# Two of three down projections of the second FFNs: one plain pair of lots, then three pairs in seven half products

## The reference, cut to what matters

```
def swiglu(x, w1, w3, w2):
    return (jax.nn.silu(x @ w1) * (x @ w3)) @ w2
...
for l in range(DEPTH):                       # DEPTH = 2, D_MODEL = 1024, D_FF = 2816
    x = x + 0.5 * swiglu(rms_norm(x, ffn1_norm[l]), ffn1_w1[l], ffn1_w3[l], ffn1_w2[l])
    ... mixing ...
    x = x + 0.5 * swiglu(rms_norm(x, ffn2_norm[l]), ffn2_w1[l], ffn2_w3[l], ffn2_w2[l])
```

## Time and profile before

| | us |
|---|---|
| span of the profiled execution | 2748.1 |
| median of the executions timed | 2749.83 |
| lowest, highest of 3 | 2749.41, 2750.02 |
| TensorE busy | 2743.3 (100%) |
| TensorE weight loads busy | 2337.2 (85%) |
| VectorE busy | 1851.7 (67%) |
| ScalarE busy | 1335.1 (49%) |
| GpSimd busy | 940.7 (34%) |

### The profile page before, as it was taken

One profiled execution on the slowest core, in us unless ns is written; L12 is line 12 of the kernel. 1 busy time (PEld: TensorE's weight loads), 2 busy tenths in 40 slices (PEclk: granted clock), 3 DMA queues, 4 the chain that ended last, 5 costly groups with the idle time before them and its releaser, 6 DMA issues.

```text
span 2748.1 us, 41845 instructions
## 1 busy us (share of the span) xinstructions
PE 2743.3 (100%) x16054; PEld 2337.2 (85%) x16054; DVE 1851.7 (67%) x2984; ACT 1335.1 (49%) x2103; POOL 940.7 (34%) x466
## 2 busy tenths in 40 slices
PE   9999999999999999999999999999999999999999
PEld 8898888777788889898998988887777888898988
DVE  7686857885667448585785878578846674585755
ACT  6353444655355346353563534446553653553533
POOL 0135824433343442131121357244333434421221
DMA  5333583222222232233332335832222222322332
GB/s 171 108 108 116 151 180 107 84 71 72 83 85 85 85 100 94 92 116 100 108 108 92 116 115 159 171 108 84 70 73 81 86 83 85 100 99 94 108 98 102
DMA packets 113110, 284.80 MB, mean 104 GB/s; under 512 B 35617, under 2 KB 45345, under 8 KB 112417
## 3 DMA queue, kind: packets, MB, share of 16 engines
q1 hardware_dynamic: 112928, 282.35, 34.6%
HBM read 268.67 MB, written 9.44 MB: 101 GB/s over the span
## 4 chain that ended last, share of the span: by engine, by line
PE 99%; DVE 1%; ACT 0%; issue 0%; DVEq 0%; ACTq 0%
PE bank L627 22%; PE bank L629 22%; PE bank L628 22%; PE bank L676 7%; PE bank L677 7%; PE bank L678 7%; PE bank L653 1%; PE bank L655 1%; PE bank L654 1%; PE bank L1048 1%; PE bank L1067 1%; PE bank L1082 1%; PE bank L817 1%; PE bank L1181 1%; PE bank L1035 0%; PE bank L1240 0%
## 5 line engine op out<-in xcount | busy, mean ns | idle before, releaser
L476 POOL TENSOR_TENSOR w_lo<-raw,w_hi 128x1024 fp32r<-128x1024 f32 x208 | 519.8, 2504 | 872.1 <-ACT w_hi L468 872.1
L627 PE MATMUL bank<-h_hi,w_hi 128*128 128x512 f32 x1504 | 593.4, 395 | 0.5 <-DVE silu_a L2363 0.3
L629 PE MATMUL bank<-h_hi,w_lo 128*128 128x512 f32 x1504 | 585.8, 390 | 0.0
L628 PE MATMUL bank<-h_lo,w_hi 128*128 128x512 f32 x1504 | 585.8, 390 | 0.0
L468 ACT ACTIVATE w_hi<-raw 128x1024 fp32r<-128x1024 f32 x310 | 326.5, 1056 | 353.8 <-PE bank L629 313.5
L541 POOL TENSOR_TENSOR w_lo<-raw,w_hi 128x1024 fp32r<-128x1024 f32 x122 | 223.4, 1854 | 802.3 <-DVE bank L2308 802.3
L627 PEld LDWEIGHTS bank<-h_hi,w_hi 128*128 128x128 f32 x1504 | 282.3, 188 | 65.6 <-issue 7.1
L629 PEld LDWEIGHTS bank<-h_hi,w_lo 128*128 128x128 f32 x1504 | 282.4, 188 | 59.8
L628 PEld LDWEIGHTS bank<-h_lo,w_hi 128*128 128x128 f32 x1504 | 282.5, 188 | 56.4
L627 PE MATMUL bank<-g_hi,w_hi 128*128 128x512 f32 x698 | 271.9, 390 | 0.0
L628 PE MATMUL bank<-g_lo,w_hi 128*128 128x512 f32 x698 | 271.7, 389 | 0.0
(11 more groups left out here) (452 smaller groups left out, 5895.7 us busy)
## 6 DMA issues: line engine op xcount, KB each, us to landing
raw<-in_w_lots SPq DMA_DIRECT2D x478, 512.0 KB, 3.7
s_wd<-s_z SPq DMA_DIRECT2D x8, 512.0 KB, 2.7
s_t<-s_taps SPq DMA_DIRECT2D x16, 256.0 KB, 12.9
da_s<-da_qk SPq DMA_DIRECT2D x16, 256.0 KB, 4.1
x<-in_x SPq DMA_DIRECT2D x8, 256.0 KB, 5.5
raw_k<-in_w_lots SPq DMA_DIRECT2D x8, 256.0 KB, 5.6
s_w_im<-s_wd SPq DMA_DIRECT2D x32, 64.0 KB, 3.9
s_w_re<-s_wd SPq DMA_DIRECT2D x32, 64.0 KB, 2.5
```

Source lines behind the costliest of these rows:

```text
L476: eng.tensor_tensor(w_lo[:, s], raw[:, s], w_hi[:, s].bitcast(f32), SUB).then_inc(S["lo_done"], 1)
L627: pe.matmul(b[:, :], w_hi[:, s, kw], xh[:, k], start=(k == 0), stop=False)
L628: pe.matmul(b[:, :], w_hi[:, s, kw], xl[:, k], start=False, stop=False)
L629: return pe.matmul(b[:, :], w_lo[:, s, kw], xh[:, k], start=False, stop=(k == nk - 1))
```

## The change

In thirds 0 and 1 of the second FFN, in both layers, the down stage becomes: one plain pair of lots, both lots side by side over the blocks of g in the order 0, 4, 1, 5, 2, 6, 3, 7; then three pairs in seven half products each, with sums of blocks of g (token halves by halves of k) in place of sums of h. The up stages keep their matmuls. In their gating, `multiply` writes into `g_whole`, which holds all eight tiles in the place of `g_lo`, and the low parts are made in place, later: pair (k, k+4) after the four gated sums of that block pair, in the last two loop turns and behind them. The gated sums and their low parts (16 operations of 256 columns for each kind) are done by VectorE, their rounding by ScalarE. The weight low parts of the halved down pairs go to POOL, as in halved up pairs; the two that VectorE made at the end of the up stage go too. Two of the gated sums, S3 and S4, lie in spare places, one of them a constant, `hgreset`, that is loaded again in layer 0. Half products of g use `g_lo`'s and `g_hi`'s own second halves of blocks 0 to 3 for the rounded S3 and S4, so those are rounded only after the plain pair.

```
+DOWN_HALVED = ((), (0, 1))
+DOWN_ORDER = (0, 4, 1, 5, 2, 6, 3, 7)
+DOWN_LEAD = 1
+GS_ORDER = S1, S2, S3, S4
...
 PE:
+            class Down:
+                x11, x12, x22 = ([blocks_of(a, k0, cols) for a in (g_hi, g_lo)] for k0, cols in ((0, one), (4, one), (4, two)))
+                sums = [[[gs_hi[j][:, k] for k in range(4)], gs_lo[j]] for j in S_SUMS]
...
+                def ready(self, j):
+                    pe.wait_ge(S["c_ones_g_lo"], LOADED + gs_at(self.which, self.th, GS_ORDER.index(j)))
...
-            def q5(n):
+            def q5(n, x):
                 pe.wait_ge(S["x3_in_xcopy"], xcopy_at(n) - 1)
                 pe.wait_ge(S["w0_in_t_lo"], t_at(n, T1))
+                x.ready(S1)
...
-            def q7(n):
+            def q7(n, x):
                 pe.wait_ge(S["x5_in_yv"], y_at(n))
+                x.ready(S3)
...
+            def down_halved(which, th, n, g0):
+                for j in range(2):
+                    begin(n + j, 0, OUT[n + j])
+                for i, k in enumerate(DOWN_ORDER):
+                    pe.wait_ge(S["g_done"], g0 - KT + i + 1)
+                    for j in range(2):
+                        m = passes(bank[OUT[n + j] % 4], slot(n + j), k, g_hi, g_lo, k, KT)
+                        if k == KT - 1:
+                            m.then_inc(S["out_done"], 1)
...
+                halved(n + 2 * DOWN_LEAD, n + KT, Down(which, th))
...
 ScalarE:
+            def round_gs(which, th, j, g0):
+                act.wait_ge(S["x4_in_g_sum"], 2 * LOADED + gs_at(which, th, 3))
+                if j in (S1, S2):
+                    act.wait_ge(S["gated_done"], g0)
+                else:
+                    act.wait_ge(S["out_done"], OUT[FIRST_LOT[which][th] + 2 * KT + 2 * DOWN_LEAD])
+                for k in range(4):
+                    ins = act.activation(gs_hi[j][:, k], gs_sum[j][k], AFT.Copy)
+                ins.then_inc(S["x6_in_g_hi"], 1)
...
+            def down_halved(which, th, n, g0):
+                d = n + 2 * DOWN_LEAD
+                round_t(d, T1)
+                round_t(d, T3)
+                high(act, d + 1, 4)
+                round_gs(which, th, S1, g0)
+                round_t(d, T2)
+                round_gs(which, th, S2, g0)
+                round_t(d, T4)
+                round_gs(which, th, S3, g0)
+                copy_x(d)
+                round_gs(which, th, S4, g0)
+                for a in range(d, n + KT, 2):
+                    high(act, a + 2)
+                    if a > d:
+                        copy_x(a)
+                    round_weights(a + 2, a)
...
 VectorE:
+            def sums_of_g(which, th, k, g):
+                V.wait_ge(S["gated_done"], g + k + 4 + 1)
...
+                s1 = do(TT(gs_sum[S1][k], a21, a22, SUB))
+                do(TT(gs_sum[S3][k], a11, a21, SUB))
+                need(s1)
+                chain(TT(gs_sum[S2][k], gs_sum[S1][k], a11, SUB))
+                TT(gs_sum[S4][k], a12, gs_sum[S2][k], ADD).then_inc(S["x4_in_g_sum"], 1)
...
+            def low_gs(which, th, j):
+                V.wait_ge(S["x6_in_g_hi"], 2 * LOADED + gs_at(which, th, GS_ORDER.index(j)))
+                for k in range(4):
+                    ins = TT(gs_lo[j][k], gs_sum[j][k], gs_hi[j][:, k].bitcast(f32), SUB)
+                ins.then_inc(S["c_ones_g_lo"], 1)
...
+            def down_halved(which, th, n):
+                d = n + 2 * DOWN_LEAD
+                add_t(d, T1)
+                add_t(d, T3)
+                low_t(d, T1)
+                add_t(d, T2)
+                low_t(d, T3)
+                low_t(d, T2)
+                add_t(d, T4)
+                low_t(d, T4)
+                low_gs(which, th, S1)
+                low_gs(which, th, S2)
+                for j in range(2 * DOWN_LEAD):
+                    down(n, j, 0)
+                low_gs(which, th, S3)
+                for a in range(d, n + KT, 2):
+                    i = a - n
+                    if a > d:
+                        down_v(a - 2, i - 2)
+                        down_w(a - 2, i - 2)
+                    add_t(a + 2, T1)
+                    add_t(a + 2, T3)
+                    low_t(a + 2, T1)
+                    if a > d:
+                        down_y(a - 2, i - 2)
+                    else:
+                        low_gs(which, th, S4)
+                        take_down_y(a, i)
+                    add_t(a + 2, T2)
+                    low_t(a + 2, T3)
+                    low_t(a + 2, T2)
+                    add_t(a + 2, T4)
+                    if a > d:
+                        take_down_y(a, i)
+                        down_x(a - 2, i - 2)
+                    low_t(a + 2, T4)
...
 VectorE, halved (up stage), with whole = this third's down stage is halved:
+                    if whole:
+                        pass
+                    elif i > i0 + 1:
                         low_g(i - 2, g0)
...
+                    if whole and i - 2 >= KT // 2:
+                        sums_of_g(1, th, i - 2 - KT // 2, g0)
+                        lows_of_g(th, i - 2 - KT // 2, g0)
                 a = n + 2 * J - 2
                 take_v(a, J - 1)
                 need(done[J % 2])
-                multiply(J - 2, g0)
+                multiply(J - 2, g0, whole)
                 take_w(a, J - 1)
-                low_g(J - 2, g0)
+                if whole:
+                    sums_of_g(1, th, J - 2 - KT // 2, g0)
+                else:
+                    low_g(J - 2, g0)
                 take_first(a, J - 1)
                 take_x(a, J - 1)
+                if whole:
+                    lows_of_g(th, J - 2 - KT // 2, g0)
                 need(done[(J - 1) % 2])
-                multiply(J - 1, g0)
+                multiply(J - 1, g0, whole)
+                if whole:
+                    sums_of_g(1, th, J - 1 - KT // 2, g0)
+                    lows_of_g(th, J - 1 - KT // 2, g0)
+                    return
```

More of the change, by code:

```diff
@@ new lines, in blocks_of, with __init__, ready @@
+            def blocks_of(whole, k0, cols):
+                return [whole[:, k0 + k, cols] for k in range(4)]
+            one, two = slice(0, HALF), slice(HALF, SEQ)
+            class Up:
+                x11, x12, x22 = ([blocks_of(a, k0, cols) for a in (h_hi, h_lo)] for k0, cols in ((0, one), (4, one), (4, two)))
+                sums = [[blocks_of(a[j], 0, one) for a in (s_hi, s_lo)] for j in range(4)]
+                def ready(self, j):
[3 more added lines that the diff above has]
+                sums = [[[gs_hi[j][:, k] for k in range(4)], gs_lo[j]] for j in S_SUMS]
+                def __init__(self, which, th):
+                    self.which, self.th = which, th
+                def ready(self, j):
+                    pe.wait_ge(S["c_ones_g_lo"], LOADED + gs_at(self.which, self.th, GS_ORDER.index(j)))
@@ L717, in q7, with halved @@
+            def q7(n, x):
                 pe.wait_ge(S["x5_in_yv"], y_at(n))
[L718 to L724, removed]
+                x.ready(S3)
+                with_sums(x_bank(n), n, T3, x.sums[S3]).then_inc(S["x1_in_prod"], 1)
+            def halved(first, to, x):
+                for a in range(first, to, 2):
+                    q1(a, x)
@@ L1650, in three_plain @@
             def three_plain(n, g, which):
+                whole = 0 in DOWN_HALVED[which]
                 high_sum(2 * which)
@@ L1657, in three_plain @@
                 silu(n, 0, g)
[L1658 removed]
+                round_g(0, g, whole)
                 high(act, n + 6)
@@ L1689, in six_plain, with halved @@
                 silu(n + 10, 1, g)
-            def halved(n, i0, J, g0):
+            def halved(n, i0, J, g0, whole=False):
                 for i in range(i0, J):
@@ L2446, in six_plain, with halved @@
                 low_g(4, g)
-                whole(n + 10, 5)
+                pair_of_plain(n + 10, 5)
                 multiply(5, g)
-            def halved(n, i0, J, g0):
+            def halved(n, i0, J, g0, th=None):
+                whole = th is not None
                 for i in range(i0, J):
@@ L2457, in halved @@
                             need(done[i % 2])
-                            multiply(i - 2, g0)
+                            multiply(i - 2, g0, whole)
                         take_w(a - 2, i - 1)
```

206 lines of the change are left out of this document (131 added, 75 removed).

## The result

The changed kernel takes 2783.48 us (median of 4 runs, 2782.73 to 2783.75) against 2749.93 for the kernel before on the same chip: a ratio of 1.0121, interval 1.0107 to 1.0135, so 33.5 us slower. The forecast was 2770 us, slower; the direction and the mechanism came out, the size fell short by 13 us.

What follows compares the result with a forecast made beforehand. TensorE's matmul count times spacing bounds the kernel, unless another engine comes late. Per site -2.5 + 0.7 + 2.6 + 3.2 + 0.25 = +4.25 us, four sites +17, restarts 3: +20, forecast 2770 us, range 2757 to 2784.

Steps and rivals of the forecast that it cites:

- the clock rival: Products 7 and 1 behind the second stall run at half clock: 11.5 us more in all, 2781 us, chance 0.11.
- The gain on TensorE: Down stages: narrow half products replace wide matmuls, 41.0 us for 43.5, gaining 2.5 us a site, 10 in all.
- Stall 0.7 us: End of the up stage: last half product waits 0.7 us for an evacuation behind VectorE's new sums and lows.
- Stall 2.6 us: Down stage, product 5: low parts of S1 come at +14.8 us, TensorE needs them at 12.3; 2.6 us a site.
- The eight T steps: VectorE's T weight sums ahead of S1's low parts: 6.0 us alone, 6.85 with ScalarE's interleaved roundings.
- Stall 3.2 us: Down stage, product 7: Y's take-over, behind S4 in VectorE's queue, is done at +22.4, TensorE waits from 19.2.
- 0.25 us at the next product 7: Next halved down pair: a leftover wait of 0.25 us a site while VectorE catches up.
- Restarts, 3 us: After each halt TensorE's restart costs 0.25 us; 12 halts, 3 us in all.
- The narrow operations' price: VectorE's 256-column operations start 0.33 us apart, against 0.60 for 512 columns.
- the prediction's rule: Contrary rule, not followed: narrow VectorE operations start 0.42 us apart, 2.5 us a site more, 2780 us.
- all hidden: Rival: VectorE, busy 18 us of 40 in the down stretch, hides all new work; 2740 us, chance 0.09.
- half-way: Rival: VectorE's queue is about 3 us shorter, stalls 2.5 to 4 us a site; 2750 to 2756 us, chance 0.10.

Runs made afterwards that it cites:

- the experiment: Changed kernel plus 40 useless matmuls of 256 columns between products 2 and 7 of each site's first halved down pair, keeping TensorE busy: 2778.15 us.
- the second edit with one plain pair: Against the first reordered kernel (2772.69 us): ScalarE's copy of W ahead of T2's rounding, low T4 behind S1 to S3, starting POOL: 2774.14 us.

## Why the prediction was right, and by how much it fell short

The measured 2783.48 us lies above the band that the prediction gave its own forecast, 2759 to 2778, and 0.5 us under the upper end of the range, which was that wide only because it took in a fall of the clock. The queue was right, but that the time comes so near the 2781 of the clock rival is luck: that rival had the clock at 11.5 us and POOL at nothing.

- **The gain on TensorE**, 2.5 us a site. Right: narrow matmuls with g start 0.119 us apart at full clock, the plain pair takes 10.91.
- **"Stall 0.7 us" at the end of the gating.** Right in place and size, 0.74 at each site. But moving its cause away gained nothing, so as a term of a sum it belongs with the stall behind it.
- **"Stall 2.6 us" before product 5.** Right: 2.51 to 2.57. VectorE's low parts of S1 were forecast by +14.8 us, and product 5 started at 1132.08, +14.9 into the down stage. The eight T steps took 6.83 us, forecast 6.85.
- **"Stall 3.2 us" before product 7.** The step that failed. It took the low parts of S4 at 1.34 us, the price of S3's. They took 4.11. The prediction had said that POOL takes the two weight lows "3.66 us, as now", at no cost to VectorE; it counted POOL's time and not what POOL keeps others from. With POOL held back the wait was 3.05 and 3.17 us. Four sites make 10.4 us of the 13.
- **0.25 us at the next product 7.** Not there: after such a long wait VectorE had caught up. 1 us too much.
- **Restarts, 3 us.** At full clock the very next start after a wait comes 0.08 to 0.10 us late (0.19 to 0.22 in place of 0.12), and those behind it then stand mostly 0.113 to 0.118 apart and make most of that up; nearly all of the 3 us was not there.
- **"The clock falls"**, a rival at 0.11 and 11.5 us. It happened, at all four sites, at a net cost of about 8 us; the experiment, which holds it behind product 7 alone, gives 5.3 to 7.0. The error was to set it beside the forecast as a case of its own. In these runs it fell at every wait of over 4 us, at some of 2.6 us and at none of up to 1.6 us, so the two errors come together. The Trainium skill, "TensorE: Matmul & The Clock Gate", Part 1, by which an idle array falls to 1.2 GHz, agrees with the second and third windows above: TensorE is busy for 0.22 of 5.80 us, and then the granted clock is 0.50.
- **The narrow operations' price.** 0.33 from start to start, as taken: eight low parts in 2.77 us. The 2.5 us a site more of the prediction's rule did not come. The Trainium skill, "VectorE: DVE Perf Modes", section "The DRAIN you can't avoid", says beside that rule that a next operation that is not held starts earlier, which the prediction left out; the trace agrees with that.
- **The rivals "all hidden" and "half-way"** fell: both wait groups are there four times.

The sum closes, with the clock's part an estimate: 20.2 us forecast, less 4 for restarts and the next product 7, less 1 for up stages that were a little better, plus 10.4 for POOL and 7.8 for the clock, is 33.4 us, against 33.5 measured.

## What to carry to other kernels

Where work is added to a queue that is in order, its cost is set by what stands behind it and when that is due, not by the engine's busy share: with three halved pairs VectorE was 70% busy and it cost 33 us, with two halved pairs behind 22 us of cover it was 71% busy and cost nothing. For three pairs, another order or holding POOL back won 9 to 12 us of the 33. Price each operation with its neighbour on the other engine, too, and lay POOL's work beside VectorE operations that read PSUM. And a stall that is long enough brings the next loss, the clock, with it: add the two, don't list them as alternatives.

## What was not expected of the hardware

**VectorE stops while POOL subtracts, if both its inputs are in SBUF.** Narrow low parts, 0.41 us each alone, went at one for each of POOL's instructions (2.04 and 1.48 us above); one narrow `scalar_tensor_tensor` went from 0.42 to 2.52. The sums T2 and T4 and all T low parts, which have one operand in PSUM, keep their 0.69 beside it; T1 and T3, with both in SBUF, meet a subtraction of POOL in none of these kernels. This timeline of VectorE after, then of POOL, is the case with nothing lost:

```profile
1125.11 0.69 DVE L2432 TENSOR_TENSOR t_lo<-bank,t_hi 128x512 fp32r<-128x512 f32 x1
```

```profile
1125.13 3.66 POOL L567 TENSOR_TENSOR w_lo<-raw,w_hi 128x1024 fp32r<-128x1024 f32 x2 [24.70 <-DVE bank L2418]
```

The Trainium skill, "SBUF — State Buffer", section "Who interferes with whom", has this rule: a VectorE instruction with two SBUF inputs and a GpSimd instruction that reads SBUF exclude each other, whichever starts second waits for the other's end, and with at most one SBUF input, outside VectorE's two-port modes, it is free of it. These rows agree with it. The prediction had not drawn on that rule.

**The clock also fell after waits of 2.6 us**, in some sites and not in others: with POOL held back at the last two, with S4 behind Y at the first two, and in the second edit with one plain pair at three of four. Where and how often it falls differs between runs with nearly the same waits, and the spread of the run with POOL held back, 2768.72 to 2774.67, may come from that; this was not tested. The four kernels without a wait over 1.6 us in the sites kept 1.00 there.

**What stays open** is whether three halved pairs can be made to pay. Two orders were tried, 2772.69 and 2774.14 us, and neither did.
